# Second operands of the PEER top-k chain placed in PSUM, in a two-block transformer kernel

## The chip, the cores and the metric

One NeuronCore of a Trainium2 chip runs the whole program. The metric is the device time of one execution in microseconds. A profile of one execution gives each engine's instructions: PE (TensorE matmuls) with PEld (its weight loads), DVE (VectorE), ACT (ScalarE), POOL (GpSimd) and SP (SyncE, which issues most DMAs).

## What is computed

The reference runs two transformer blocks on 256 tokens of width 1024. The change lies in the feed-forward part of the first one, PEER: each of 8 heads scores two sets of 128 keys, takes the best 16 of each, adds them pairwise, takes the best 16 pairs, and each pair names one of 16,384 experts.

```python
s = jnp.einsum('thpd,hpkd->thpk', q, sub_keys)
s_top, i_top = lax.top_k(s, P_TOPK)
cand = s_top[..., 0, :, None] + s_top[..., 1, None, :]
best, ci = lax.top_k(cand.reshape(P_CHUNK, P_HEADS, P_TOPK * P_TOPK), P_TOPK)
e1 = jnp.take_along_axis(i_top[..., 0, :], ci // P_TOPK, axis=-1)
e2 = jnp.take_along_axis(i_top[..., 1, :], ci % P_TOPK, axis=-1)
gate = jax.nn.softmax(best.astype(jnp.float32), axis=-1).astype(xc.dtype)
act = jax.nn.gelu(jnp.einsum('thkd,td->thk', u_tab[expert], xc), approximate=False)
return jnp.einsum('thk,thkd->td', gate * act, v_tab[expert])
```

## The kernel before

The kernel does not gather experts. It writes the 16,384 experts as a grid of 128 by 128 (first key, second key), computes all of them column by column, and multiplies by a gate grid that is zero where an expert was not chosen. So the choice of experts need not be known when the first columns are computed, and the kernel uses that: while DVE chooses, TensorE computes the activations of the first 44 columns.

The five engines run one instruction list each, in the order in which the code issues it, and meet only by semaphores. What matters around the change:

- **TensorE** projects the queries and scores the keys (two score tiles of 128 tokens, `sc`), waits until ACT has copied all scores out of PSUM (L805), and then runs `top_u` (L808 to L824) for 44 columns into PSUM banks psD[0] and psD[1]. A column is 16 matmuls at L817, with the rounded weights, and 8 at L823, with what the rounding left; those 8 wait for `u_lo_ready`. Then it waits for the last GELU (L832), then for `chosen_ready`, and transposes the chosen keys and gates of each 128-token tile (L838) into psD[1] and psD[2].
- **ACT** rounds the weights of a column (`top_hi`), and takes the GELU of each two columns (L1403). After the 15th and the 20th of these GELUs it computes the exponential of a tile's best scores (L1411), for which it waits for `dmax_ready`.
- **POOL** computes what the rounding left of each column, one subtraction of 128x1024 in SBUF (L1677), 44 times.
- **DVE** makes the choice, for tiles t = 0 and 1 one after the other (loop at L1921). The steps of a tile: `top16` on 16 rows of scores (max, index, replace, max, index); the *table* step L1926, which turns the indices `si` into floats `sf`; the *candidate* sums L1932, four `tensor_tensor`; `top16` on 8 rows of candidates; the difference L1944 for the exponential; then the *key* steps L1963 to L1978. These find the row of each chosen candidate by comparing its position with the row starts (L1967, 128 x 16 = 2048 elements), multiplying by key differences (L1954 in `pick_key`) and summing (L1969), split the sum into key and start with casts, a shift and a mask (L1970 to L1974), and do the same once more for the second key (L1975, L1976, L1954, L1978). Behind both tiles come two `gate_norm` (L1910), each of which waits for ACT's exponential and ends with `chosen_ready`; then the copies of the transposed tiles to `pick` (L1983).
- After `pick`, TensorE runs the middle columns (L857, into psY) between gate matmuls (L873), while POOL and DVE build the one-hot operands of these (L1685, L1689, L2004, L2005).

All operands of the DVE steps lie in `arena` or `cst`, in SBUF. psY and psD are the two halves of PSUM, of four banks of 512 floats each. While `top_u` runs, psD[2], psD[3] and psY hold nothing that is still needed once all scores are copied. Most later steps (columns with 12 matmuls at L897, the second block, its experts) follow one another on TensorE; expert weights are loaded when a slot comes free (L548 to L554).

`seq` issues an instruction and makes DVE wait for its end, `mark` only counts it.

Of the kernel before, what the change touches and what calls it, by code (L numbers as in the profile page):

```python
# [22 lines left out]
U32 = mybir.dt.uint32  # L23
ALU = mybir.AluOpType
# [3 lines left out]
P = 128  # L28
D = 1024
T = 256  # L30
TT = T // P
# [11 lines left out]
PH, TOPK, NKEYS = 8, 16, 128  # L43
# [158 lines left out]
def build(nc, w, out):  # L202
# [3 lines left out]
    with ExitStack() as ctx:  # L206
# [3 lines left out]
        def sem(name):  # L210
            return ctx.enter_context(nc.semaphore(name))
# [45 lines left out]
        psD = [psD_all[:, 512 * i:512 * (i + 1)] for i in range(4)]  # L257
        psY = ctx.enter_context(nc.psum_tensor("psY", [P, 2048], F32))
# [3 lines left out]
        row_at, row_step = cst[:, 642:658], cst[:, 658:674]  # L262
        rope_tab = cst[:, 384:640]

        def vcol(name, i=0, n=1):
            return vec[:, VEC[name][0] + i:VEC[name][0] + i + n]

        def ar(at, *shape):
            n = int(np.prod(shape))
            v = arena[:, at:at + n]  # L270
            if len(shape) == 2:
                v = v.rearrange("p (a b) -> p a b", a=shape[0])
            if len(shape) == 3:
                v = v.rearrange("p (a b c) -> p a b c", a=shape[0], b=shape[1])
            return v
# [21 lines left out]
        R0 = TOPU * T  # L297
        sc = ar(R0, TT, 16, NKEYS)
        sc2 = ar(R0 + 4096, 16, NKEYS)
        sv, sf = ar(R0 + 6144, TT * 16, TOPK), ar(R0 + 6656, TT * 16, TOPK)  # L300
        si = ar(R0 + 7168, TT * 16, TOPK).bitcast(U32)
        cand = ar(R0 + 7680, TT * PH, CANDS)
        cand2 = ar(R0 + 11776, PH, CANDS)
        cpos, cdec = ar(R0 + 9216, P), ar(R0 + 9344, 2, P).bitcast(U32)
        dkey = ar(R0 + 9600, PH, TOPK)
        best, ci = ar(R0 + 13824, TT * PH, TOPK), ar(R0 + 14080, TT * PH, TOPK).bitcast(U32)
        cjf = ar(R0 + 14592, TT * PH, TOPK)
        chosen = ar(R0 + 15360, 3, TT * PH * TOPK)
        eqa = ar(R0 + 16384, PH * TOPK, TOPK)
        qpT = ar(0, 16, T)  # L310
        gate_all = ar(0, NKEYS, T)
        conv_w = pick[:].rearrange("p a t -> p (a t)")[:, 0:K * TAPS]
# [105 lines left out]
        sc_ready = sem("sc_ready")  # L418
# [1285 lines left out]
        def _(dve):  # L1704
            step = [0]

            def seq(ins):

                step[0] += 1
                ins.then_inc(dve_step, 1)  # L1710
                dve.wait_ge(dve_step, step[0])

            def mark(ins):
                step[0] += 1
                ins.then_inc(dve_step, 1)
                return step[0]
# [5 lines left out]
            tt, ts, stt = nc.vector.tensor_tensor, nc.vector.tensor_scalar, nc.vector.scalar_tensor_tensor  # L1722
# [78 lines left out]
            i = STATS.index("mean")  # L1801
# [37 lines left out]
            for n in range(n_units + 1):  # L1839
# [4 lines left out]
                if n:  # L1844
                    i = n - 1
# [26 lines left out]
            for m in range(4):  # L1872
                ps = take(TILE["out"] + m)
                for j in range(2):
                    k = 2 * m + j
# [25 lines left out]
            def top16(src, spare, vals, idx):  # L1901

                seq(nc.vector.max(vals[:, 0:8], src))
                mark(nc.vector.max_index(idx[:, 0:8], vals[:, 0:8], src))
                seq(nc.vector.match_replace(spare, vals[:, 0:8], src, NEG))
                seq(nc.vector.max(vals[:, 8:16], spare))
                mark(nc.vector.max_index(idx[:, 8:16], vals[:, 8:16], spare))
# [13 lines left out]
            for t in range(TT):  # L1921
                dve.wait_ge(sc_ready, t + 1)
                for hp in range(16):
                    top16(sc[:, t, hp, :], sc2[:, hp, :], sv[:, 16 * t + hp, :], si[:, 16 * t + hp, :])
                dve.wait_ge(dve_step, step[0])
                seq(nc.vector.tensor_copy(sf[:, 16 * t:16 * (t + 1), :], si[:, 16 * t:16 * (t + 1), :]))  # L1926
                hv = sv[:, 16 * t:16 * (t + 1), :].rearrange("p (h b) k -> p h b k", b=2)
                at = 0
                for lo, hi, n in ROWS:

                    dst = cand[:, PH * t:PH * (t + 1), at:at + (hi - lo) * n].rearrange("p h (i j) -> p h i j", j=n)
                    last = mark(tt(dst, hv[:, :, 0, lo:hi].rearrange("p h (i a) -> p h i a", a=1)  # L1932
                                   .broadcast_to([P, PH, hi - lo, n]),
                                   hv[:, :, 1, 0:n].rearrange("p h (a j) -> p h a j", a=1)
                                   .broadcast_to([P, PH, hi - lo, n]), ALU.add))
                    at += (hi - lo) * n
                dve.wait_ge(dve_step, last)
                for h in range(PH):
                    top16(cand[:, PH * t + h, :], cand2[:, h, :], best[:, PH * t + h, :], ci[:, PH * t + h, :])
                dve.wait_ge(dve_step, step[0])  # L1940

                bt = best[:, PH * t:PH * (t + 1), :]
                gt = chosen[:, 2, t * P:(t + 1) * P].rearrange("p (h k) -> p h k", h=PH)
                tt(gt, bt, bt[:, :, 0:1].broadcast_to([P, PH, TOPK]), ALU.subtract).then_inc(dmax_ready, 1)  # L1944

                cit = ci[:, PH * t:PH * (t + 1), :].rearrange("p h k -> p (h k)")
                cj = cjf[:, PH * t:PH * (t + 1), :].rearrange("p h k -> p (h k)")
                hf = sf[:, 16 * t:16 * (t + 1), :].rearrange("p (h b) m -> p h b m", b=2)
                dve.wait_ge(sc_ready, TT)
                eq = eqa.rearrange("p (h k) m -> p h k m", h=PH)  # L1950

                def pick_key(values):

                    seq(tt(eq, eq, values.rearrange("p h (a m) -> p h a m", a=1).broadcast_to([P, PH, TOPK, TOPK]),  # L1954
                           ALU.mult))

                def along(a):
                    return a.rearrange("p (n a) -> p n a", a=1).broadcast_to([P, PH * TOPK, TOPK])

                def each(a):  # L1960
                    return a.rearrange("p (a m) -> p a m", a=1).broadcast_to([P, PH * TOPK, TOPK])

                mark(tt(dkey[:, :, 1:], hf[:, :, 0, 1:], hf[:, :, 0, 0:TOPK - 1], ALU.subtract))  # L1963
                mark(nc.vector.tensor_copy(dkey[:, :, 0:1], hf[:, :, 0, 0:1]))
                seq(nc.vector.tensor_copy(cpos, cit))
                mark(tt(dkey, dkey, row_step.rearrange("p (a m) -> p a m", a=1).broadcast_to([P, PH, TOPK]), ALU.add))
                seq(tt(eqa, along(cpos), each(row_at), ALU.is_ge))  # L1967
                pick_key(dkey)
                seq(nc.vector.tensor_reduce(cj, eqa, AX.X, ALU.add))  # L1969
                seq(nc.vector.tensor_copy(cdec[:, 0, :], cj))  # L1970
                mark(ts(cdec[:, 1, :], cdec[:, 0, :], 7, None, ALU.logical_shift_right))
                seq(ts(cdec[:, 0, :], cdec[:, 0, :], NKEYS - 1, None, ALU.bitwise_and))
                mark(nc.vector.tensor_copy(chosen[:, 0, t * P:(t + 1) * P], cdec[:, 0, :]))
                seq(nc.vector.tensor_copy(cj, cdec[:, 1, :]))  # L1974
                seq(tt(cj, cpos, cj, ALU.subtract))  # L1975
                seq(tt(eqa, each(iota[:, 0:TOPK]), along(cj), ALU.is_equal))  # L1976
                pick_key(hf[:, :, 1, :])
                seq(nc.vector.tensor_reduce(chosen[:, 1, t * P:(t + 1) * P], eqa, AX.X, ALU.add))  # L1978
# [114 lines left out]
            for c in range(4):  # L2093
                n = MAIN - 4 + c
# [42 lines left out]
            for m in range(4):  # L2137

                ps = take(TILE["qks"] + m).rearrange("p (a t) -> p a t", a=2)
                dst = (qs if m < 2 else ks)[:, 2 * (m % 2):2 * (m % 2) + 2, :]  # L2140
# [47 lines left out]
            for kind, n in second_order():  # L2188
                i = TILE.get(f"{kind}{n}")
# [17 lines left out]
                elif kind == "f":  # L2207
                    dve.wait_ge(blk2["sig"], 1)
                    for k in range(4):
                        last = mark(ts(fh[:, k, :], fh[:, k, :], lbv[:, 5, k:k + 1], lbv[:, 3, k:k + 1],  # L2210
                                       ALU.mult, ALU.add))
# [23 lines left out]
            for level in range(8):  # L2235
# [5 lines left out]
                for i in range(4):  # L2241
                    ps = take(TILE[f"level{level}"] + i).rearrange("p (h c q) -> p h c q", h=2, c=2)
                    h0 = 4 * (i // 2) + i % 2
                    dst = Sc[:, h0:h0 + 3:2, :].rearrange("p h (c q) -> p h c q", c=3)[:, :, 0:3:2, :]
                    m = ident if level == 0 else lmask[:, level - 1, :]
                    for j in range(2):
                        mb = m.rearrange("p (a q) -> p a q", a=1).broadcast_to([P, 2, P])
                        if level == 0:
                            last = tt(dst[:, j], ps[:, j], mb, ALU.mult)
                        else:  # L2250
                            last = nc.vector.copy_predicated(dst[:, j], mb, ps[:, j])
# [11 lines left out]
            for hp in range(4):  # L2263
                last = mark(ts(gh[:, hp, :], gh[:, hp, :], vcol("hg_g", hp), None, ALU.mult))
# [16 lines left out]
            for m in range(4):  # L2281
                ps = take(TILE["out2"] + m)
                for j in range(2):
                    k = 2 * m + j
# [152 lines left out]
            for k in range(K):  # L2437
                dve.wait_ge(x_ready, 4 * K + k + 1)
                last = mark(ts(hT[:, k, :], xT[:, k, :], vcol("final_g2", k), None, ALU.mult))
# [6 lines left out]
            for i in range(4):  # L2446
                lo, hi = OUT_AT[i], OUT_AT[i + 1]
# [122 lines left out]
```

## Time and profile before

| | |
|---|---|
| median of 3 runs | 1778.1 us (1776.81 to 1781.54) |
| the profiled execution | 1776.78 us, span 1775.0 us, granted TensorE clock 0.992 |
| PE busy | 1724.2 us, 97% of the span |
| PEld busy | 1358.4 us, 77% |
| DVE busy | 1023.3 us, 58% |
| ACT busy | 642.6 us, 36% |
| POOL busy | 288.0 us, 16% |

Busy shares are averages over the whole span. What an edit is worth is read from the stretch in which it lies: which engine waits there, and for what. The granted clock is a share of TensorE's full 2.4 GHz; 0.50 means 1.2 GHz.

### The profile page before, as it was taken

How to read it: one execution, taken by the hardware profiler on the slowest of the kernel's cores; microseconds unless marked ns; L12 is line 12 of the kernel's file. 1: busy time of each engine (PE TensorE's matmuls, PEld its weight loads, DVE VectorE, ACT ScalarE, POOL GpSimd, SP SyncE). 2: the span in 40 equal slices, each digit the busy share in tenths (PEclk: the TensorE clock that was granted, in tenths of full speed). 3: DMA queues.
4: the chain of work that ended last, by engine and by line, in shares of the span. 5: the costliest groups of instructions: out<-in, count | busy, mean ns of one | idle time of the engine just before them, and what ended most of it. 6: DMA issues, size and time to landing. Idle time of an engine off the chain costs nothing.

```text
span 1775.0 us, 24252 instructions
## 1 busy us (share of the span) xinstructions
PE 1724.2 (97%) x9242; PEld 1358.4 (77%) x9242; DVE 1023.3 (58%) x2021; ACT 642.6 (36%) x916; POOL 288.0 (16%) x155
## 2 busy tenths in 40 slices
PE   7999999999999899999999999999999999899997
PEld 4877766778999799877788888888877888655454
DVE  2779565220899788887777776777523642412223
ACT  2121454011445366433345555545346230221221
POOL 1010000021698699310000000000000000000000
PEclk9999999999999899999999999999999999999998
DMA  9365321333544122455555555555613226599995
GB/s 389 145 269 220 151 95 48 136 126 120 199 180 166 48 96 95 142 190 189 189 174 187 186 188 190 187 189 205 271 58 133 101 102 271 199 420 427 426 428 210
DMA packets 33341, 343.68 MB, mean 194 GB/s; under 512 B 3953, under 2 KB 4593, under 8 KB 5361
## 3 DMA queue, kind: packets, MB, share of 16 engines
q1 hardware_dynamic: 31968, 339.78, 51.0%
q10 hardware_dynamic: 1296, 2.84, 0.4%
q8 instruction: 53, 0.87, 0.2%
q14 instruction: 24, 0.19, 0.0%
HBM read 340.51 MB, written 2.10 MB: 193 GB/s over the span
## 4 chain that ended last, share of the span: by engine, by line
PE 92%; DMA 3%; DVE 3%; issue 1%; ACT 1%; SPq 0%; DVEq 0%; PEldq 0%
PE psD L606 30%; PE psY L897 20%; PE psD L883 6%; PE psD L1121 5%; PE psY L857 5%; PE psD L817 5%; PE psD L873 3%; PE psD L885 3%; PE psD L1130 3%; PE psD L823 2%; DMA arena<-in_experts 2%; PE psY L758 2%; PE psY L642 1%; PE psY L606 1%; DMA ring<-in_w_mod 1%
## 5 line engine op out<-in xcount | busy, mean ns | idle before, releaser
L897 PE MATMUL psY<-ring_r,work_r 128*128 128x512 f32 x1536 | 365.9, 393 | 1.8 <-issue 1.8
L897 PEld LDWEIGHTS psY<-ring_r,work_r 128*128 128x128 f32 x1536 | 280.1, 188 | 71.7 <-issue 10.6
L1244 ACT ACTIVATE arena<-psD 128x512 f32<-128x512 f32 (+5 forms) x182 | 124.9, 690 | 464.8 <-PE psD L606 277.9
L606 PE MATMUL psD<-xh,ring 128*128 128x256 f32 x1280 | 284.7, 381 | 4.6 <-DVE xh L1894 1.5
L606 PEld LDWEIGHTS psD<-xh,ring 128*128 128x128 f32 x1280 | 240.6, 190 | 47.2 <-issue 11.0
L1244 ACT ACTIVATE ring_r<-ring 128x1024 fp32r<-128x1024 f32 x188 | 192.7, 1056 | 175.0 <-PE psY L897 115.2
L883 PE MATMUL psD<-xh_r,ring_r 128*128 128x512 f32 x480 | 171.3, 397 | 0.0
L2027 DVE TENSOR_TENSOR ring_r<-ring,ring_r 128x1024 fp32r<-128x1024 f32 x128 | 156.4, 1222 | 14.6 <-ACT ring_r L1244 14.3
L885 PE MATMUL psD<-xh_r,ring_r 128*128 128x256 f32 x480 | 134.6, 280 | 0.0
L606 PE MATMUL psD<-arena,ring 128*128 128x256 f32 (+1 forms) x560 | 127.4, 386 | 3.9 <-DVE arena L1870 1.5
L606 PEld LDWEIGHTS psD<-arena,ring 128*128 128x128 f32 x560 | 105.8, 190 | 22.8 <-issue 5.2
L883 PEld LDWEIGHTS psD<-xh_r,ring_r 128*128 128x128 f32 x480 | 90.2, 188 | 21.6
L2022 DVE TENSOR_TENSOR ring_r<-ring,ring_r 128x1024 fp32r<-128x1024 f32 x60 | 73.5, 1225 | 43.9 <-ACT ring_r L1244 43.9
L1781 DVE SCALAR_TENSOR_TENSOR arena<-arena,pick 128x256 f32<-128x256 f32 x232 | 92.8, 480 | 0.0
L885 PEld LDWEIGHTS psD<-xh_r,ring_r 128*128 128x128 f32 x480 | 90.5, 189 | 2.3
L857 PE MATMUL psY<-xh,ring 128*128 128x256 f32 x384 | 89.9, 385 | 0.9 <-DVE pick L1983 0.9
L1677 POOL TENSOR_TENSOR ring_r<-ring,work_r 128x1024 fp32r<-128x1024 f32 x30 | 77.9, 2607 | 60.4 <-ACT work_r L1244 60.4
L606 PE MATMUL psD<-arena 128*128 128x256 f32 (+3 forms) x288 | 82.1, 425 | 0.8 <-DVE arena L2113 0.8
L857 PEld LDWEIGHTS psY<-xh,ring 128*128 128x128 f32 x384 | 71.7, 194 | 10.0 <-issue 1.3
L1689 POOL TENSOR_TENSOR work<-work,pick 128x1024 f32<-128x1024 f32 x32 | 79.2, 2474 | 0.0
L873 PEld LDWEIGHTS psD<-ring,work 128*128 128x128 f32 x512 | 62.2, 192 | 1.7
L2420 DVE TENSOR_TENSOR yrow_lo<-psD,yrow_hi 64x512 fp32r<-64x512 f32 x32 | 22.0, 689 | 71.4 <-ACT yrow_hi L1244 70.9
(315 smaller groups left out, 2513.1 us busy)
## 6 DMA issues: line engine op xcount, KB each, us to landing
ring<-in_tables SPq DMA_DIRECT2D x60, 1024.0 KB, 4.9
arena<-in_experts SPq DMA_DIRECT2D x30, 2048.0 KB, 19.8
ring<-in_w_in SPq DMA_DIRECT2D x18, 2048.0 KB, 9.4
ring<-in_experts SPq DMA_DIRECT2D x18, 2048.0 KB, 17.3
ring<-in_early_v SPq DMA_DIRECT2D x34, 1024.0 KB, 5.0
ring<-in_w_mod SPq DMA_DIRECT2D x12, 2048.0 KB, 8.8
ring<-in_early_u SPq DMA_DIRECT2D x11, 2048.0 KB, 8.2
ring<-in_mid_u SPq DMA_DIRECT2D x12, 1024.0 KB, 5.0
```

The lines of the kernel that those rows point to most:

```text
L606: last = nc.tensor.matmul(dst, a, b, start=(i == 0), stop=(i == len(pairs) - 1))
L817: last = nc.tensor.matmul(ps, hi[:, k * P:(k + 1) * P], h[:, k, :], start=(k == 0 and h is h_hi), stop=False)
L857: last = nc.tensor.matmul(psY[:, 1024 + 512 * (m % 2) + j * T:1024 + 512 * (m % 2) + (j + 1) * T], col_slot[m % 3][:, at:at + P], hT[:, k, ...
L873: last = nc.tensor.matmul(psD_all[:, at:at + P], one_a[:, n % 2, i, :], one_b[:, n % 2, i, :], start=True, stop=True)
L883: nc.tensor.matmul(bank[:, :], u_hi[c % 2][:, k * P:(k + 1) * P], xh_r[:, :, k, :], start=(k == 0), stop=(k == K - 1), skip_group_check=True)
L885: last = nc.tensor.matmul(bank[:, 0:T], lo[:, k * P:(k + 1) * P], h_hi[:, k, :], start=False, stop=(k == K - 1), skip_group_check=True)
L897: last = nc.tensor.matmul(psY[:, t * D + h * 512:t * D + (h + 1) * 512], wgt[:, b, t * P:(t + 1) * P], v[:, h * 512:(h + 1) * 512], start= ...
L1121: last = nc.tensor.matmul(psD[bank][lo:lo + 64, :], lhs, wt[:, col:col + 512], start=(k == 0), stop=(k == K - 1))
L1244: return nc.scalar.activation(dst, src, f, **kw)
L1689: nc.gpsimd.tensor_tensor(one_a[:, h], one_a[:, h], g.broadcast_to([P, 8, P]), ALU.mult).then_inc(a_ready, 1)
L1781: s[j % 2] = mark(stt(acc, y[:, j:j + T], conv_w[:, m * TAPS + j:m * TAPS + j + 1], acc, ALU.mult, ALU.add))
L2027: tt(lo, a, v_hi[b].bitcast(F32), ALU.subtract).then_inc(v_lo_ready, 1)
```

## The change

For each tile, the second side of the two-operand steps moves from `arena` to PSUM. The key steps' wide array `eqa` becomes psY. The positions `cpos`, the sums `cj` and the integer pair `cdec` go into psD[2]; the first half of the sorted scores is copied there too (`sv_row`, a new copy), and so are the key differences before the row step is added (`dkey_wide`). The float indices are written to psD[3] (`sf_wide`) and copied from there to `sf` in SBUF by a new copy behind the candidate sums. A new SBUF array `cstart` takes the float start, so that the subtraction for `cj` has one operand on each side. The wait for both score tiles, which stood ahead of the first tile's key steps, stands ahead of its table step. Sizes and the number of steps stay as they are, but for the two new copies in each tile.

```diff
@@ -298,15 +298,18 @@
         sc = ar(R0, TT, 16, NKEYS)
         sc2 = ar(R0 + 4096, 16, NKEYS)
         sv, sf = ar(R0 + 6144, TT * 16, TOPK), ar(R0 + 6656, TT * 16, TOPK)
+        sf_wide = psD[3].rearrange("p (n k) -> p n k", n=TT * 16)
         si = ar(R0 + 7168, TT * 16, TOPK).bitcast(U32)
         cand = ar(R0 + 7680, TT * PH, CANDS)
         cand2 = ar(R0 + 11776, PH, CANDS)
-        cpos, cdec = ar(R0 + 9216, P), ar(R0 + 9344, 2, P).bitcast(U32)
-        dkey = ar(R0 + 9600, PH, TOPK)
+        cpos, cj = psD[2][:, 0:P], psD[2][:, P:2 * P]
+        cdec = psD[2][:, 2 * P:4 * P].rearrange("p (a n) -> p a n", a=2).bitcast(U32)
+        sv_row = psD[2][:, 0:P].rearrange("p (h k) -> p h k", h=PH)
+        dkey, cstart = ar(R0 + 9600, PH, TOPK), ar(R0 + 9728, P)
+        dkey_wide = psD[2][:, P:2 * P].rearrange("p (h k) -> p h k", h=PH)
         best, ci = ar(R0 + 13824, TT * PH, TOPK), ar(R0 + 14080, TT * PH, TOPK).bitcast(U32)
-        cjf = ar(R0 + 14592, TT * PH, TOPK)
         chosen = ar(R0 + 15360, 3, TT * PH * TOPK)
-        eqa = ar(R0 + 16384, PH * TOPK, TOPK)
+        eqa = psY.rearrange("p (n m) -> p n m", n=PH * TOPK)
         qpT = ar(0, 16, T)
         gate_all = ar(0, NKEYS, T)
         conv_w = pick[:].rearrange("p a t -> p (a t)")[:, 0:K * TAPS]
@@ -1923,17 +1926,20 @@
                 for hp in range(16):
                     top16(sc[:, t, hp, :], sc2[:, hp, :], sv[:, 16 * t + hp, :], si[:, 16 * t + hp, :])
                 dve.wait_ge(dve_step, step[0])
-                seq(nc.vector.tensor_copy(sf[:, 16 * t:16 * (t + 1), :], si[:, 16 * t:16 * (t + 1), :]))
+                dve.wait_ge(sc_ready, TT)
+                mark(nc.vector.tensor_copy(sf_wide[:, 16 * t:16 * (t + 1), :], si[:, 16 * t:16 * (t + 1), :]))
                 hv = sv[:, 16 * t:16 * (t + 1), :].rearrange("p (h b) k -> p h b k", b=2)
+                seq(nc.vector.tensor_copy(sv_row, hv[:, :, 0, :]))
                 at = 0
                 for lo, hi, n in ROWS:
 
                     dst = cand[:, PH * t:PH * (t + 1), at:at + (hi - lo) * n].rearrange("p h (i j) -> p h i j", j=n)
-                    last = mark(tt(dst, hv[:, :, 0, lo:hi].rearrange("p h (i a) -> p h i a", a=1)
+                    last = mark(tt(dst, sv_row[:, :, lo:hi].rearrange("p h (i a) -> p h i a", a=1)
                                    .broadcast_to([P, PH, hi - lo, n]),
                                    hv[:, :, 1, 0:n].rearrange("p h (a j) -> p h a j", a=1)
                                    .broadcast_to([P, PH, hi - lo, n]), ALU.add))
                     at += (hi - lo) * n
+                mark(nc.vector.tensor_copy(sf[:, 16 * t:16 * (t + 1), :], sf_wide[:, 16 * t:16 * (t + 1), :]))
                 dve.wait_ge(dve_step, last)
                 for h in range(PH):
                     top16(cand[:, PH * t + h, :], cand2[:, h, :], best[:, PH * t + h, :], ci[:, PH * t + h, :])
@@ -1944,9 +1950,7 @@
                 tt(gt, bt, bt[:, :, 0:1].broadcast_to([P, PH, TOPK]), ALU.subtract).then_inc(dmax_ready, 1)
 
                 cit = ci[:, PH * t:PH * (t + 1), :].rearrange("p h k -> p (h k)")
-                cj = cjf[:, PH * t:PH * (t + 1), :].rearrange("p h k -> p (h k)")
                 hf = sf[:, 16 * t:16 * (t + 1), :].rearrange("p (h b) m -> p h b m", b=2)
-                dve.wait_ge(sc_ready, TT)
                 eq = eqa.rearrange("p (h k) m -> p h k m", h=PH)
 
                 def pick_key(values):
@@ -1960,10 +1964,11 @@
                 def each(a):
                     return a.rearrange("p (a m) -> p a m", a=1).broadcast_to([P, PH * TOPK, TOPK])
 
-                mark(tt(dkey[:, :, 1:], hf[:, :, 0, 1:], hf[:, :, 0, 0:TOPK - 1], ALU.subtract))
-                mark(nc.vector.tensor_copy(dkey[:, :, 0:1], hf[:, :, 0, 0:1]))
+                hf_wide = sf_wide[:, 16 * t:16 * (t + 1), :].rearrange("p (h b) m -> p h b m", b=2)
+                mark(nc.vector.tensor_copy(dkey_wide[:, :, 0:1], hf[:, :, 0, 0:1]))
+                mark(tt(dkey_wide[:, :, 1:], hf_wide[:, :, 0, 1:], hf[:, :, 0, 0:TOPK - 1], ALU.subtract))
                 seq(nc.vector.tensor_copy(cpos, cit))
-                mark(tt(dkey, dkey, row_step.rearrange("p (a m) -> p a m", a=1).broadcast_to([P, PH, TOPK]), ALU.add))
+                mark(tt(dkey, dkey_wide, row_step.rearrange("p (a m) -> p a m", a=1).broadcast_to([P, PH, TOPK]), ALU.add))
                 seq(tt(eqa, along(cpos), each(row_at), ALU.is_ge))
                 pick_key(dkey)
                 seq(nc.vector.tensor_reduce(cj, eqa, AX.X, ALU.add))
@@ -1971,8 +1976,8 @@
                 mark(ts(cdec[:, 1, :], cdec[:, 0, :], 7, None, ALU.logical_shift_right))
                 seq(ts(cdec[:, 0, :], cdec[:, 0, :], NKEYS - 1, None, ALU.bitwise_and))
                 mark(nc.vector.tensor_copy(chosen[:, 0, t * P:(t + 1) * P], cdec[:, 0, :]))
-                seq(nc.vector.tensor_copy(cj, cdec[:, 1, :]))
-                seq(tt(cj, cpos, cj, ALU.subtract))
+                seq(nc.vector.tensor_copy(cstart, cdec[:, 1, :]))
+                seq(tt(cj, cpos, cstart, ALU.subtract))
                 seq(tt(eqa, each(iota[:, 0:TOPK]), along(cj), ALU.is_equal))
                 pick_key(hf[:, :, 1, :])
                 seq(nc.vector.tensor_reduce(chosen[:, 1, t * P:(t + 1) * P], eqa, AX.X, ALU.add))
```

## Rows read from the trace of the kernel before

**Rows 1.** Page, part 4: the chain that ended last, by engine.

```profile
PE 92%; DMA 3%; DVE 3%; issue 1%; ACT 1%; SPq 0%; DVEq 0%; PEldq 0%
```

**Rows 2.** Chain of waits in order of time: start us, us, what.

```profile
452.73 0.96 PE psD L823 x8
...
519.17 1.22 PE psD L823 x8
...
578.25 0.61 ACT arena L1244
578.85 6.01 issue
...
587.45 9.25 PE psY L857 x34
...
598.49 2.59 PE psY L857 x12
```

**Rows 3.** Timeline of DVE, first tile: start us, us, engine, line, operation.

```profile
471.82 0.49 DVE L1926 CAST arena<-arena 128x256 f32<-128x256 uint32 x1
472.35 3.05 DVE L1932 TENSOR_TENSOR arena<-arena 128x128 f32<-128x128 f32 x4
...
486.13 0.27 DVE L1963 TENSOR_TENSOR arena<-arena 128x120 f32<-128x120 f32 x1
...
489.18 4.37 DVE L1954 TENSOR_TENSOR arena<-arena 128x2048 f32<-128x2048 f32 x1
...
495.90 2.34 DVE L1970 CAST arena<-arena 128x128 uint32<-128x128 f32 x1
...
519.20 0.29 DVE L1903 MAX8 arena<-arena 128x8 f32<-128x128 f32 x1
```

**Rows 4.** Timeline of POOL beside the first tile's key steps.

```profile
487.03 4.37 POOL L1677 TENSOR_TENSOR ring_r<-ring,top_hi 128x1024 fp32r<-128x1024 f32 x1 [0.97 <-ACT top_hi L1244]
491.36 6.79 POOL L1677 TENSOR_TENSOR ring_r<-ring,work_r 128x1024 fp32r<-128x1024 f32 x2
```

**Rows 5.** Timeline of DVE, second tile.

```profile
544.76 5.39 DVE L1932 TENSOR_TENSOR arena<-arena 128x128 f32<-128x128 f32 x4
...
561.48 0.27 DVE L1963 TENSOR_TENSOR arena<-arena 128x120 f32<-128x120 f32 x1
...
575.90 0.21 DVE L1972 TENSOR_SCALAR arena<-arena 128x128 uint32<-128x128 uint32 x1
...
579.20 2.29 DVE L1954 TENSOR_TENSOR arena<-arena 128x2048 f32<-128x2048 f32 x1
...
583.85 0.29 DVE L1915 TENSOR_REDUCE gate_sum<-arena 128x8 f32<-128x128 f32 x1
```

**Rows 6.** L1994 on DVE: duration ns min/median/max, first and last start us.

```profile
L1994 DVE TENSOR_TENSOR arena<-psD,arena x32: 901/920/930, 601.2 to 729.5; 128x352 f32 x30, 128x352 f32<-128x352 f32 x2
```

**Rows 7.** DVE groups by form, whole span: busy us, mean ns, idle before.

```profile
L1842 DVE TENSOR_REDUCE row_max<-psD 128x1 f32<-128x512 f32 x32 | 22.1, 689 | 19.2 <-PE psD L606 19.1
...
L1862 DVE TENSOR_TENSOR arena<-psD,arena 128x512 f32<-128x512 f32 x8 | 5.5, 692 | 16.7 <-PE psD L606 16.7
...
L2229 DVE TENSOR_TENSOR arena<-arena 128x512 f32<-128x512 f32 x7 | 4.8, 685 | 0.8 <-ACT arena L1244 0.8
...
L1827 DVE COPY arena<-psD 128x256 f32<-128x256 f32 x8 | 3.4, 425 | 7.3 <-PE psD L773 7.3
...
L2398 DVE MEMSET psY<- 128x2048 f32 x1 | 1.8, 1765 | 0.5 <-DVE arena L2396 0.5
```

**Rows 8.** Timeline of ACT: the second tile's exponential.

```profile
569.37 0.31 ACT L1244 ACTIVATE arena<-arena 128x128 f32<-128x128 f32 x1
```

**Rows 9.** Busy time by stretch: length, PE, PEld, DVE, ACT, POOL, granted clock, DMA.

```profile
580.00:582.00 2.00, 0.00 (x0) 0.00 (x0) 1.97 (x2) 0.00 (x0) 0.00 (x0) 0.65 0.00 0
...
590.00:592.00 2.00, 2.00 (x8) 1.67 (x8) 2.00 (x2) 0.52 (x1) 2.00 (x2) 0.79 0.00 0
...
730.00:730.50 0.50, 0.00 (x0) 0.00 (x0) 0.47 (x2) 0.50 (x2) 0.00 (x0) 1.00 1.17 492
```

## The prediction, written before the change was run

> **What bounds the kernel now.** I read the page's chain first, then the chain of waits around the edited lines, then the DVE and POOL timelines of that stretch. TensorE holds 92% of the chain [rows 1], so DVE work counts only where TensorE stands still for it. In order of time there is one such place. TensorE runs the 44 early columns of L817 and L823 until 578.25 us; ACT's last GELU ends at 578.86; then come 6.01 us marked "issue", to 584.86, the transposes of L838, and at 587.45 the start of L857 [rows 2]. "Issue" says that the profile names no releaser. The code does: L835 waits for chosen_ready, which the first `gate_norm` raises, and that `gate_norm` stands on DVE's queue directly behind the second tile's key steps, which end at 583.85 [rows 5]. So the end of the DVE chain decides about 6 us, and nothing else of that chain is on the path.
>
> Why is the chain that long? In the first tile casts and shifts of 128 elements at L1970 to L1975 take some 2.34 us each, six in a row [rows 3]; in the second tile the same line L1972 takes 0.21 [rows 5]. L1954 takes 4.37 in one place and 2.29 in another [rows 3, 5]. POOL's splits explain it: two of them end at 491.36 + 6.79 = 498.15, and the cast that began at 495.90 ends at 498.24, just behind them [rows 3, 4]. It goes both ways: POOL's split at 487.03 takes 4.37 because L1967 was running [rows 4]. The two engines exclude each other for whole instructions, when DVE reads two SBUF operands or does a plain cast or shift within SBUF. With one operand in PSUM that is not so: L1994 (psD with arena) ran 32 times beside POOL's gate products and took 901 to 930 ns, never one POOL instruction longer [rows 6].
>
> **The change, part by part**, all on DVE's queue, for each of two tiles:
> 1. *Table.* The four sums of L1932 take 3.05 and 5.39 us [rows 3, 5]. Their first operand moves to PSUM, so at about 0.3 each (L1963: 0.27 for 120 elements [rows 3]) they cost 1.2. The cast of L1926 (0.49, [rows 3]) writes PSUM now and costs what a 256-element PSUM copy costs, 0.43 [rows 7]: no difference worth a term. Added are `sv_row` (0.3) and the copy back to `sf` (0.43). Saved: 3.05 - 1.9 = 1.1 and 5.39 - 1.9 = 3.5.
> 2. *Keys and candidates.* These run from 486.13 to 519.20, 33.1 us, in the first tile, and from 561.48 to 583.85, 22.4, in the second [rows 3, 5]. Afterwards there are the same six wide steps of 2048 elements and ten narrow ones. Every two-input step has one PSUM side and every cast or shift at least one, so none should wait for POOL: 6 x 2.3 (L1954 undisturbed [rows 5]) + 10 x 0.29 = 16.7. Saved: 16.4 and 5.7.
> 3. *The moved wait* for all scores now stands before the first tile's cast at 471.82 [rows 3]. TensorE itself waits for those score copies before L817, and it is in L817's columns by 452.7 [rows 2]: cost nothing, with 19 us of cover.
> 4. No queue of SP or POOL gets or loses an instruction, and no DMA moves.
>
> Sum for the chain: 1.1 + 3.5 + 16.4 + 5.7 = 26.7, so the key steps end near 583.9 - 26.7 = 557 instead of 583.9.
>
> The unknown price is a wide step that reads and writes PSUM in one instruction (L1967, L1954, L1976 now all write psY): no row shows one. Below: a PSUM fill of 2048 takes 1.77, less than 2.29 [rows 7]; that bound would only add to a slack that is not on the path. Above: L1994's 920 ns for 352 elements, 2.61 ns each [rows 6], would make 5.35 of 2.3. I take 2.3, because L1994 steps through arena by whole columns, while a contiguous sum with one PSUM input takes 692 for 512 elements against 685 with two SBUF inputs [rows 7].
> The Trainium skill speaks against the change here (VectorE: DVE Perf Modes, section on the TRN2 errata): it gives a fixed cost of 120 cycles for an instruction from PSUM and 58 from SBUF. At its 0.96 GHz and some 23 touched instructions a tile, that is an estimated 3 us on the chain, whose key steps would end at 560 instead of 557; the pair 692 and 685 does not show it.
>
> *What is late next.* The second `gate_norm` also needs ACT's exponential, which ends at 569.37 + 0.31 = 569.68 by ACT's own order [rows 8]; both norms are over by about 571. That is before TensorE's last column and ACT's GELU at 578.86, which end the wait from then on. So the chain has 20 us of room, and only 6.01 of the 26.7 reaches the path.
>
> On the path:
> - the wait: -6.0 [rows 2];
> - transposes, pick copies and issue from 584.86 to 587.45, 2.59 us at the lowered clock; I put 2.2 at the full one: -0.4;
> - the clock. The granted clock falls to 0.65 in 580 to 582, TensorE idle since 578.25; it is back at full only within 590 to 592, where it averages 0.79 [rows 9]. The first 34 matmuls of L857 take 9.25, while later 12 take 2.59, so 34 should take 7.34 [rows 2]: -1.9. After the change TensorE pauses for some 0.7, transposes, and pauses for about 1. From 730.00 to 730.50 TensorE is idle throughout and the clock stays at 1.00 [rows 9]; I take that as the nearest row;
> - L823 waits now and then for a POOL split that DVE held up: the piece at 519.17 takes 1.22 where others take 0.96 [rows 2], and there are three such pieces, together -0.7.
>
> Sum: 6.0 + 0.4 + 1.9 + 0.7 = 9.0. The profiled execution took 1776.8 us (span 1775.0), which becomes 1767.8; it is 1.3 below the median of the runs, 1778.1, and from that the sum gives 1769.1. I forecast **1769**.
>
> **Rivals.**
> - *The clock still falls* over the shorter pauses. For: transposes are thin work. Against: the row at 730. The 1.9 and 0.4 go, the gain is 6.7, 1771.4.
> - *It does not free the chain*, or the gain is given back. PSUM steps could wait for POOL all the same (the casts that write PSUM still read SBUF, and no row shows one beside POOL), or the expert stage, where DMA carries much of its 3% of the chain [rows 1], could have its own pace. Against: L1994's even times; and expert loads are issued as slots come free (L548), so they move with the work ahead of them. The time stays at about 1778.
> - *Slower: in-place wide steps in PSUM are slow.* The place is L1954, L1967, L1976 and the two reductions. With 12 wide steps the chain is back at its old end when each takes 2.3 + 26.7/12 = 4.5, and the time is worse by over 0.3% (5.3 us, about what a measurement of this kernel can tell from no change) from 2.3 + 32/12 = 5.0. At 5.35 the chain ends 12 x 3.05 - 26.7 = 9.9 later; less 0.7, that is 1787.3. The mechanism would be one bank serving read and write by turns; the 32 reductions of L1842 read 512 PSUM elements in 0.69 each, and a fill is fast [rows 7], so both sides alone are cheap. The Trainium skill (PSUM — Partial Sum Buffer, section on bank collisions) calls each bank of a partition a RAM of its own and gives no rate for one engine doing both; no run here shows it.
>
> **How the numbers follow.** Forecast 0.68, clock falls 0.17, no gain 0.10, slower 0.05. A gain under 5.3 us can also come out of the second case by scatter, so faster 0.83, same 0.12, slower 0.05. The range: down to 1766, where the profiled execution's own sum (1767.8) lies with some room for a shorter transposing step; up to 1773, which holds the second case and about 1.6 us of a chain or a clock that comes out worse. Outside lie no gain, slower, and little else.
>
> **What would show it.** Right: L1970 to L1975's successors near 0.3 us in both tiles, L1954 near 2.3 four times, POOL's splits all near the same length, the second tile's last reduction long before 578, a pause of under 1 us before L838, L857's first 34 matmuls in about 7.4 us and a granted clock at 1.00 throughout. A clock of 0.5 there with a short pause means the second case. Wrong: wide PSUM steps at 4 us or more, or narrow steps that still end just behind a POOL split; then chosen_ready comes last again.

## The result, and the profile after

The changed kernel takes 1769.93 us (median of 5 runs, 1769.36 to 1770.89) against 1778.1: ratio 0.995, interval 0.9936 to 0.9965. That is 8.2 us less. The forecast was 1769 in a range of 1766 to 1773.

The profiled execution of it has a span of 1767.8 us, against 1775.0. Its lines lie 3 further down in the front part of the file and up to 5 further down from the table step on: L820 and L826 are the column matmuls L817 and L823, L841 the transposes, L860 the middle columns, L1680 POOL's split; L1930, L1937, L1958, L1983 and L1988 on DVE are L1926, L1932, L1954, L1978 and L1983. The chain of waits, start and us, answers to [rows 2]:

```profile
454.58 0.96 PE psD L826 x8
...
579.42 0.61 ACT arena L1247
...
580.07 0.56 PE psD L841 x3
...
580.65 1.03 DVE pick L1988 x2
...
581.97 7.58 PE psY L860 x34
```
The 6.01 us of "issue" are gone: ACT's GELU ends at 580.03 and the transposes start at 580.07. From the first L823 piece to the end of the first 34 middle matmuls it was 452.73 to 596.70, 143.97 us; now it is 454.58 to 589.55, 134.97. That is 9.0 us less. Behind that point the two executions are alike: 1775.0 - 596.7 = 1178.3 and 1767.8 - 589.55 = 1178.25. Nothing is given back later. Ahead of it the execution of after is 1.85 us late (454.58 against 452.73), and that is not the change: in a third profile of the changed kernel the same piece starts at 452.91. Busy time by stretch (length, five engines, granted clock, DMA), first of the kernel before, then of the changed one:

```profile
36.00:38.00 2.00, 1.72 (x8) 1.57 (x9) 2.00 (x8) 0.00 (x0) 0.00 (x0) 1.00 0.96 410
```
```profile
36.00:38.00 2.00, 1.56 (x5) 1.36 (x6) 2.00 (x7) 0.00 (x0) 0.00 (x0) 0.76 1.00 426
38.00:40.00 2.00, 2.00 (x6) 1.55 (x6) 1.09 (x3) 0.00 (x0) 1.30 (x1) 0.50 1.01 369
```
Around the short pause near 36 us the clock fell in one execution and not in the other, on the same instructions. Behind the pause at 580 it stayed at 1.00 in this profile, where [rows 9] has 0.65 and 0.79 around the old one:

```profile
582.00:584.00 2.00, 2.00 (x10) 1.77 (x11) 1.98 (x2) 0.04 (x1) 1.88 (x2) 1.00 0.00 0
```

DVE in the first tile (start us, us), answering to [rows 3], and two of POOL's entries beside it:

```profile
473.65 0.43 DVE L1930 CAST psD<-arena 128x256 f32<-128x256 uint32 x1
...
485.86 2.20 DVE L1950 TENSOR_TENSOR arena<-arena 128x128 f32<-128x128 f32 x1
487.99 0.16 DVE L1968 COPY psD<-arena 128x8 f32<-128x8 f32 x1
...
491.10 2.30 DVE L1958 TENSOR_TENSOR psY<-psY,arena 128x2048 f32<-128x2048 f32 x1
...
495.77 0.30 DVE L1975 CAST psD<-psD 128x128 uint32<-128x128 f32 x1
...
496.63 0.29 DVE L1978 CAST arena<-psD 128x128 f32<-128x128 uint32 x1
...
502.15 2.29 DVE L1983 TENSOR_REDUCE arena<-psY 128x128 f32<-128x2048 f32 x1
```
```profile
483.12 4.80 POOL L1680 TENSOR_TENSOR ring_r<-ring,work_r 128x1024 fp32r<-128x1024 f32 x2 [0.96 <-ACT work_r L1247]
...
491.28 2.41 POOL L1680 TENSOR_TENSOR ring_r<-ring,work_r 128x1024 fp32r<-128x1024 f32 x1
```
No step with a side in PSUM is held any more: the product at 491.10 and the split at 491.28 run side by side, and both take their usual time. The wide steps take 2.30, the casts of 128 elements 0.28 to 0.30, and the key steps run from 487.99 to 504.44, 16.5 us instead of 33.1. The exception is L1950, the former L1944, which the change left with two SBUF inputs: 2.20 us for 128 elements. It ends at 488.06, just behind the two splits that end at 487.92 (483.12 + 4.80), as the old steps did. The cast L1930 of 256 elements takes 0.43 in both tiles; undisturbed in SBUF, in the second tile of before, it took 0.29:

```profile
544.43 0.29 DVE L1926 CAST arena<-arena 128x256 f32<-128x256 uint32 x1
```

In the second tile of the changed kernel:

```profile
541.91 1.37 DVE L1950 TENSOR_TENSOR arena<-arena 128x128 f32<-128x128 f32 x1
543.20 0.16 DVE L1968 COPY psD<-arena 128x8 f32<-128x8 f32 x1
...
557.36 2.29 DVE L1983 TENSOR_REDUCE arena<-psY 128x128 f32<-128x2048 f32 x1
...
571.10 0.29 DVE L1918 TENSOR_REDUCE gate_sum<-arena 128x8 f32<-128x128 f32 x1 [10.49 <-ACT arena L1247]
```
The last key step ends at 559.65. Behind the first gate norm DVE waits 10.49 us for ACT's exponential, and both gate norms are over at 572, 8 us ahead of the last GELU. POOL is freed too; a group of 30 of its 44 splits (ns min/median/max) before and after:

```profile
L1677 POOL TENSOR_TENSOR ring_r<-ring,work_r x30: 2347/2404/4446, 437.6 to 573.5; 128x1024 fp32r<-128x1024 f32 x30
```
```profile
L1680 POOL TENSOR_TENSOR ring_r<-ring,work_r x30: 2336/2408/2477, 439.3 to 572.1; 128x1024 fp32r<-128x1024 f32 x30
```

### The profile page after: what moved, and what is told of

Its sections match the earlier page's. It is cut to its first block, busy times and chain, and to the rows that moved or that the text cites. A ratio compares the mean times of both kernels' runs of the same rounds, so it can differ in the third digit from the quotient of the medians.

```text
span 1767.8 us, 24258 instructions
## 1 busy us (share of the span) xinstructions
PE 1722.2 (97%) x9242; PEld 1357.4 (77%) x9242; DVE 996.8 (56%) x2025; ACT 642.3 (36%) x916; POOL 275.8 (16%) x155
## 4 chain that ended last, share of the span: by engine, by line
PE 93%; DMA 3%; DVE 3%; ACT 1%; issue 1%; SPq 0%; DVEq 0%; PEldq 0%
PE psD L609 31%; PE psY L900 20%; PE psD L886 6%; PE psD L1124 5%; PE psD L820 5%; PE psY L860 5%; PE psD L876 3%; PE psD L888 3%; PE psD L1133 3%; PE psD L826 2%; DMA arena<-in_experts 2%; PE psY L761 2%; PE psY L645 1%; PE psY L609 1%; DMA ring<-in_w_mod 1%; PE psD L776 1%
## 5 line engine op out<-in xcount | busy, mean ns | idle before, releaser
L1247 ACT ACTIVATE arena<-psD 128x512 f32<-128x512 f32 (+5 forms) x182 | 124.8, 689 | 466.1 <-PE psD L609 279.9
L2032 DVE TENSOR_TENSOR ring_r<-ring,ring_r 128x1024 fp32r<-128x1024 f32 x128 | 156.3, 1221 | 14.6 <-ACT ring_r L1247 14.3
L860 PE MATMUL psY<-xh,ring 128*128 128x256 f32 x384 | 88.3, 379 | 1.0 <-DVE pick L1988 1.0
L1680 POOL TENSOR_TENSOR ring_r<-ring,work_r 128x1024 fp32r<-128x1024 f32 x30 | 72.1, 2406 | 66.7 <-ACT work_r L1247 66.7
L860 PEld LDWEIGHTS psY<-xh,ring 128*128 128x128 f32 x384 | 70.5, 190 | 9.5 <-issue 1.2
L876 PE MATMUL psD<-ring,work 128*128 128x128 f32 x512 | 62.3, 275 | 0.0
```

What stands on the lines that cost most here:

```text
L860: last = nc.tensor.matmul(psY[:, 1024 + 512 * (m % 2) + j * T:1024 + 512 * (m % 2) + (j + 1) * T], col_slot[m % 3][:, at:at + P], hT[:, k, ...
L876: last = nc.tensor.matmul(psD_all[:, at:at + P], one_a[:, n % 2, i, :], one_b[:, n % 2, i, :], start=True, stop=True)
L1247: return nc.scalar.activation(dst, src, f, **kw)
L2032: tt(lo, a, v_hi[b].bitcast(F32), ALU.subtract).then_inc(v_lo_ready, 1)
```

## The experiments

**Is it the exclusion by POOL, or PSUM itself?** The kernel before, with POOL's splits replaced by fills with zero, so that it leaves out the remainders of the early columns' weights:

```diff
-                nc.gpsimd.tensor_tensor(top_column(ring_r, c % 12), top_column(ring, c % 12), top_hi[c % 3].bitcast(F32),
-                                        ALU.subtract).then_inc(u_lo_ready, 1)
+                nc.gpsimd.memset(top_column(ring_r, c % 12).bitcast(F32), 0.0).then_inc(u_lo_ready, 1)
```

> The kernel before, with POOL's 44 subtractions replaced by 44 fills with zero of the same columns (the remainders of the early columns' weights are left out); every DVE operand stays in SBUF. Theory (DVE and POOL exclude each other, and PSUM only gets DVE out of that): with no POOL instruction reading SBUF beside it, L1954 takes 2.3 us all four times, two-operand steps of 128 elements 0.3, and casts and shifts 0.2 to 0.3 unless they meet a fill that excludes them too; the key steps end some 20 us earlier and the time falls by 8 to 9 us, as with the change (ratio 0.995). Rival (the steps are slow for their SBUF operands as such, and PSUM is faster): L1954 stays near 4.4, casts near 2.3, and the time stays at that of before.

Measured: 1769.84 us, ratio 0.995 (0.9935 to 0.9965), the same as the change, with every operand in SBUF. DVE, and two of the 44 fills on POOL:

```profile
487.35 0.69 DVE L1964 CAST arena<-arena 128x128 f32<-128x128 uint32 x1
...
490.61 2.29 DVE L1953 TENSOR_TENSOR arena<-arena 128x2048 f32<-128x2048 f32 x1
...
495.25 0.23 DVE L1969 CAST arena<-arena 128x128 uint32<-128x128 f32 x1
```
```profile
487.00 0.95 POOL L1677 MEMSET ring_r<- 128x1024 f32 x1 [1.44 <-ACT work_r L1244]
490.36 0.95 POOL L1677 MEMSET ring_r<- 128x1024 f32 x1 [2.41 <-ACT top_hi L1244]
```
L1953 (the old L1954) takes 2.29 instead of 4.37, though it begins at 490.61 in the middle of a fill; casts take 0.23, and up to 0.69 where they meet a fill of 0.95: the one at 487.35 ends at 488.04, just behind the fill that ends at 487.95. So the steps were never slow for lying in SBUF. They waited for POOL. A product with two SBUF inputs waits for POOL's reading, not for its writing; a cast waits for either. The Trainium skill (SBUF — State Buffer, section Who interferes with whom) describes this: a second input comes through a read port that GpSimd shares, and the faster form of a copy takes the whole shared pair. The runs agree on both.

**Which operands matter?** Two runs undo a part of the change each. First the wide array:

```diff
-        eqa = psY.rearrange("p (n m) -> p n m", n=PH * TOPK)
+        eqa = ar(R0 + 16384, PH * TOPK, TOPK)
```

> The changed kernel with only the wide array eqa back in SBUF, at its old place. Theory: what counts is two SBUF inputs of one instruction. The comparisons L1972 and L1981 have one input in PSUM and stay at 2.3 us, the sums at 2.3; only the two products of a tile (L1958) have two SBUF inputs again and take up to 4.4 where a POOL split runs. The chain ends at most 8.4 us later than with the change, at about 568, still before the last GELU at 580: the time stays at that of the change (ratio 0.995). Rival (the wide arrays in PSUM are what brings the gain): the chain ends after 580 and most of the 8 us are lost (ratio 0.998 or more).

Measured: 1770.56 us, ratio 0.9953 (0.9938 to 0.9968): nothing is lost. DVE's two products of the first tile, and POOL beside them:

```profile
492.59 2.36 DVE L1958 TENSOR_TENSOR arena<-arena 128x2048 f32<-128x2048 f32 x1
...
501.36 2.75 DVE L1958 TENSOR_TENSOR arena<-arena 128x2048 f32<-128x2048 f32 x1
```
```profile
492.79 6.81 POOL L1680 TENSOR_TENSOR ring_r<-ring,work_r 128x1024 fp32r<-128x1024 f32 x2
...
501.91 4.46 POOL L1680 TENSOR_TENSOR ring_r<-ring,work_r 128x1024 fp32r<-128x1024 f32 x1
```
The products take 2.36 and 2.75 here, less than the 4.4 that was allowed for, because they began just ahead of a split; it is POOL that waits (6.81 for two splits that take 4.8 undisturbed, 4.46 for one). Counted from the first L826 piece the key steps end only 0.4 us later than with the change. Then the integer pair:

```diff
-        cdec = psD[2][:, 2 * P:4 * P].rearrange("p (a n) -> p a n", a=2).bitcast(U32)
+        cdec = ar(R0 + 9856, 2, P).bitcast(U32)
```

> The changed kernel with only the integer pair cdec back in SBUF. Theory: casts and shifts with both sides in SBUF are excluded by POOL too, though they have one input. In each tile four steps (shift, mask, two casts) lie within SBUF again; those that meet a POOL split take up to 2.4 us, the others 0.21 to 0.23; the cast that fills cdec from PSUM stays at 0.3. The chain ends up to 10 us later, at most at about 570, and the time stays at that of the change (ratio 0.995). Rival (only instructions with two tensor inputs are excluded): all of these stay below 0.35.

Measured: 1769.25 us, ratio 0.9948 (0.9932 to 0.9963). DVE, and POOL beside it:

```profile
495.57 0.29 DVE L1975 CAST arena<-psD 128x128 uint32<-128x128 f32 x1
495.90 1.04 DVE L1976 TENSOR_SCALAR arena<-arena 128x128 uint32<-128x128 uint32 x1
496.85 0.21 DVE L1977 TENSOR_SCALAR arena<-arena 128x128 uint32<-128x128 uint32 x1
497.10 2.31 DVE L1978 CAST arena<-arena 128x128 f32<-128x128 uint32 x1
```
```profile
494.44 2.41 POOL L1680 TENSOR_TENSOR ring_r<-ring,work_r 128x1024 fp32r<-128x1024 f32 x1 [0.96 <-ACT work_r L1247]
496.84 2.50 POOL L1680 TENSOR_TENSOR ring_r<-ring,top_hi 128x1024 fp32r<-128x1024 f32 x1
```
The cast from PSUM takes 0.29. The shift of L1976 ends at 496.94, behind a split that ends at 496.85 (494.44 + 2.41), and the cast at 497.10 takes 2.31, behind the split that ends at 499.34. One-input steps within SBUF are held too, and the key steps end 5.0 us later than with the change. Undoing either of these two parts alone costs no time, because the chain has more room than that. What the other parts would cost alone, and what both together, was not run.

**How much room?** The second comparison of the second tile is repeated (L1982 there):

```diff
-                seq(tt(eqa, each(iota[:, 0:TOPK]), along(cj), ALU.is_equal))
+                for _ in range(7 if t else 1):
+                    seq(tt(eqa, each(iota[:, 0:TOPK]), along(cj), ALU.is_equal))
```

> The changed kernel with the second comparison of the second tile (L1981, 2.3 us) issued six more times in a row; it writes the same values again. Theory (the chain has 18 us of room before the last GELU): the key steps end 14.0 us later, near 573.7, both gate norms are over by about 576, TensorE's pause stays at 2.6 us, and the time stays at that of the change (ratio 0.995). Rival (the chain is still on the path): 14 us slower than the change, ratio 1.003.

Measured: 1769.66 us, ratio 0.9942 (0.9927 to 0.9957). On DVE:

```profile
554.12 16.27 DVE L1982 TENSOR_TENSOR psY<-cst,psD 128x2048 f32<-128x2048 f32 x7
...
576.62 0.29 DVE L1921 TENSOR_TENSOR arena<-arena,gate_sum 128x128 f32<-128x128 f32 x1
```
With 14 us more, the second gate norm ends at 576.91, ahead of the last column's end, and the time does not move. With 15 in place of 7:

> The same comparison issued fourteen more times. Theory: the key steps end 32.6 us later, near 592.3, the first gate norm near 593.4, so TensorE waits 13 to 14 us longer than with the change; the granted clock falls in that pause, which costs 2 us more. Time of the change plus 15 to 16 us, about 1785.5 (ratio 1.0045). If the chain had no room at all it would be 32.6 us and the clock, 1804; if another wait held TensorE anyway, no change.

Measured: 1784.41 us, ratio 1.0033 (1.0019 to 1.0046), 14.6 above the changed kernel of the same job. In the chain of waits:

```profile
579.91 13.30 issue
593.21 1.70 PE psD L841 x6
...
595.79 9.81 PE psY L860 x34
```
32.6 us of work cost 13.3 us of wait and the clock: the first 34 middle matmuls take 9.81. The first gate norm ended at 560.61 in the profile of the change; 32.6 later is 593.2, where the transposes start. So the end of the chain decides only once its room of some 19 us is used up, and in this run the rest came through whole. The forecast was 15 to 16 above the change; against the profile of the change in the same job, in which the clock fell as well (below), the stage is 14.5 us longer, against the first profile 16.2.

**Is the clock a term of its own?** The kernel before, with fill matmuls in the wait:

```diff
             pe.wait_ge(early_ready, TOPU // 2 + 2)
+            keep(12, psD[3])
```

> The kernel before, with 12 matmuls of 128x512 (the helper keep, into the unused bank psD[3]) put into TensorE's wait between the last GELU and the first transpose; DVE's chain is untouched. Theory (wait and clock are two terms): the fills of some 0.46 us each end before chosen_ready, so TensorE still starts the transposes when the DVE chain ends, but the granted clock stays at 1.00, the first 34 matmuls of L857 take 7.4 us instead of 9.25 and the transposes and copies some 0.4 less: about 2.0 us faster than before (ratio 0.999), and no more. Rival (the clock falls or rises for another reason, or its loss is covered by a later wait): the time stays at that of the kernel before, with 9.25 us for those 34 matmuls.

Measured: 1780.25 us, ratio 1.0009 (1.0 to 1.0018): not faster, and by the medians 1.9 us slower. A fill was mis-sized: it is two rows of the profile (L672) and takes 0.88 us, not 0.46:

```profile
578.37 0.61 ACT arena L1245
...
579.02 10.57 PE psD L672 x24
...
591.27 7.58 PE psY L858 x34
```
The fills last 10.57 us, past the end of the chain, and hold the transposes up. What they were to show is there all the same: 7.58 us for the 34 matmuls, not 9.25. With 6 fills:

> The kernel before with 6 instead of 12 fill matmuls in TensorE's wait. A fill is two rows of 0.44 us in the profile of the run with 12, so six last 5.3 us and end near 584.3, just ahead of chosen_ready. Theory: the DVE chain still decides when the transposes start (near 585), but the granted clock stays at 1.00 behind them and the first 34 matmuls take 7.6 us instead of 9.25: 2.0 us faster than before (ratio 0.999), the rest of the 8 to 9 us stays lost. Rival (the clock is not a term of its own): the time of the kernel before.

Measured: 1776.55 us, ratio 0.9988 (0.9979 to 0.9997). TensorE in order of time:

```profile
580.69 5.42 PE L672 MATMUL psD<-cst 128*128 128x512 f32 x12 [0.69 <-ACT arena L1245]
586.60 0.55 PE L839 MATMUL psD<-cst,arena 128*128 128x128 f32 x3 [0.49 <-DVE arena L1919]
...
588.88 7.58 PE L858 MATMUL psY<-xh,ring 128*128 128x256 f32 x34 [0.90 <-DVE pick L1984]
```
The fills end at 586.11, the transposes still wait for gate_norm, and the matmuls take 7.58. So some of the old kernel's time hung on the clock alone: 1.67 us at these matmuls, 1.9 in the medians, of which the interval leaves 0.5 to 3.7.

**Does the shorter pause keep the clock?** Not always. The changed kernel was run in two more jobs.

> The changed kernel once more, beside the following kernels on the same chip. Expected: ratio 0.995 to the kernel before; the pause between the last column and L860 stays near 2.6 us, with the granted clock at 1.00.

Measured: 1769.8 us, ratio 0.9947 (0.9933 to 0.9961). The chain, and busy time by stretch with the granted clock third from the end:

```profile
579.90 0.61 ACT arena L1247
...
582.46 9.26 PE psY L860 x34
```
```profile
582.00:584.00 2.00, 1.54 (x5) 1.27 (x5) 1.65 (x3) 0.00 (x0) 1.38 (x1) 0.69 0.00 0
584.00:586.00 2.00, 2.00 (x6) 1.64 (x5) 2.00 (x2) 1.05 (x2) 2.00 (x2) 0.50 0.00 0
```
The pause is as short as in the first profile, and the clock falls nevertheless: 9.26 us for the 34 matmuls.

> The changed kernel a third time, in the same job: ratio 0.995 to before. In the first profile of it the granted clock stayed at 1.00 over the pause before L860 and in the second it fell to 0.5; the pause is 2.6 us either way, and the first 34 matmuls take 7.6 or 9.3 us accordingly.

Measured: 1770.0 us, ratio 0.9955 (0.9942 to 0.9967), again with 9.26 and a clock of 0.50 from 582 to 584. Over the profiles in which the pause is that short (the change three times, and the fill, wide, integer and six-more runs), the clock fell there in 2 of 7.

**What is late next?** The transposes move ahead of the last column, and their waits with them (POOL's wait for the last GELU, TensorE's before its first gate matmul and the bank numbers on DVE are part of it):

```diff
-            for c in range(TOPU % 12):
+            for c in range(TOPU % 12 - 1):
                 top_u(TOPU // 12, c)
-            pe.wait_ge(early_ready, TOPU // 2 + 2)
...
+            top_u(TOPU // 12, TOPU % 12 - 1)
```

> The changed kernel with the six transposes ahead of the last of the 44 columns instead of behind the last GELU, into psD[3] and psD[2]; the copies to pick then run beside that column, and L860 starts right behind it. POOL waits for the last GELU before its first gate operand, TensorE before its first gate matmul. Theory (what is late next is GELU, transposes and copies, 2.6 us of pause): chosen_ready is there near 572, the last column starts near 576.5, so the pause of 2.6 us shrinks to the 0.6 us of the transposes: 2.0 us faster than the change, about 1767.9 (ratio 0.994). Rival (the gate stage is paced by POOL or DVE, which start only behind the last GELU): its first gate matmuls come no earlier and the time stays at that of the change.

Measured: 1767.25 us, ratio 0.993 (0.9917 to 0.9944). The second job:

> The kernel with the early transposes once more, for its interval beside the changed kernel. Expected: L860's counterpart starts right behind the last column, 2.2 us earlier than with the change, ratio 0.993 to before. If the gain over the change was scatter, the ratio comes out at 0.995.

Measured: 1766.42 us, ratio 0.9931 (0.9918 to 0.9943). Its chain:

```profile
577.86 0.65 PE psD L839 x6
...
580.43 0.96 PE psD L826 x8
581.39 7.34 PE psY L857 x34
588.73 1.78 PE psD L877 x16
```
The pause is gone; L857 there starts at once behind the last column. From the first piece of remainder matmuls, at 455.94 in this run, to the first gate matmul at 588.73 it is 132.8 us, 2.2 less than with the change. The medians are 2.6 and 3.6 below the changed kernel of the same jobs; the intervals of the ratios overlap, but 9 of its 11 runs lie below 1768.12, the fastest of the 10 runs of the change in these two jobs. Against the kernel before, it is clear of the interval in both. Its first profile, of the slowest of its five runs (1769.39), shows that one fall of the clock can take such a gain back. The window lies behind a pause of 1.82 us that every run has, the one at 730 from which the prediction took its nearest row:

```profile
722.00:724.00 2.00, 2.00 (x7) 1.62 (x8) 2.00 (x3) 0.43 (x1) 0.00 (x0) 0.72 0.21 86
```
There the clock stayed at 1.00 in the profiles of the change and fell in this one, and the first 37 matmuls behind the pause take 10.57 us, 8.99 in the second profile.

## Why the prediction came out

- *The place.* Right: the wait of 6.01 us at L838 belonged to the DVE chain, and the runs with six and with fourteen more comparisons show from which length on.
- *The cause.* Right: exclusion between DVE and POOL. It was read from ends that coincide; the fills on POOL show it by taking POOL's reads away.
- *The chain, 26.7 us.* The key steps end at 559.65, in an execution that is 1.85 late, instead of 583.85: 26.0 saved. The key steps themselves gave 16.6 and 5.9 (forecast 16.4 and 5.7), the table steps 1.6 and 3.8 (forecast 1.1 and 3.5), because four sums take 0.95 and not 1.2. Overlooked was L1944, which kept two SBUF inputs: 0.42 and 1.01 us before, 2.20 and 1.37 after. That it cost no time is owed to the room, not to the forecast.
- *The unknown price.* A wide step that reads and writes PSUM takes 2.30; the value taken was 2.3, and the slower rival falls with it. The fixed cost that the Trainium skill gives for PSUM (VectorE: DVE Perf Modes, section on the TRN2 errata) is not seen: two-input steps of 128 elements take 0.29 or 0.30 either way. Casts are dearer with PSUM: 0.28 to 0.30 against 0.21 to 0.23 undisturbed in SBUF for 128 elements, 0.43 (L1930) against 0.29 for 256. The difference doubles with the size, so it is a slower rate and not a fixed cost.
- *The terms on the path.* The wait: 6.0 and 6.0. Transposes and copies: 0.4 forecast, 1.90 instead of 2.59, so 0.7. Late splits: 0.7 forecast; from the first L823 piece to the last column's end it was 125.5 and is 124.8, so 0.7.
- *The clock, 1.9.* The size was right (1.67 in the first profile, 1.9 in the medians of the run with 6 fills), but the step "I take that as the nearest row" failed. It made of the short pause a case that either holds or does not, with 0.17 for a fall. The same kernel does both, and even the pause taken as the nearest row lost the clock in one later profile. In the two profiles with a fall the stage is 7.3 us shorter than before (the rival with the fall had 6.7), in the first 9.0, and the medians of three jobs, 8.2, 9.0 and 8.4 us, lie in that span.
- *Luck.* That the median of the first job lies 0.9 us from the forecast is in part luck: one fall of the clock moves an execution by more than that.

## What to carry to other kernels

If steps of one engine take far longer than usual and end just behind another engine's instruction, look at what the two share before moving work. Here one operand in PSUM took DVE steps out of POOL's way: at the same rate for two-input steps (2.30 against 2.29), a little dearer for casts (0.29 against 0.22). Only the part of a saving that reaches the next wait counts: 26 us of chain were worth 6 here, so look up what is late next, and move that too.

## Not expected

Short pauses of TensorE cost the clock in some executions and not in others: at a pause of 2.6 us in 2 of 7 profiles, around one of 1.3 us near 36 us in 10 of all 13, and behind a pause of 1.8 us in one. A fall cost 1.6 to 1.7 us at the two later places (10.57 against 8.99 us for 37 matmuls, 9.26 against 7.58 for 34). Near 36 us, before any edit takes effect, the first remainder piece starts 1.5 to 3.4 us later in profiles with a fall (454.38 to 456.09 against 452.73 to 452.91). What decides it was not tried, and stays open. A single profile can be off by one such fall, which can be more than the early transposes gain.
